# One core, split-precision matmuls: in the first FFN turn the products of each up unit come ahead of the modulation sums, and their columns one unit later

## The reference, cut to what matters

```
c_act = silu(c)
mod = (c_act @ w_ada + b_ada).reshape(bsz, 6, 1024)        # w_ada: 1024 x 6144
shift1, scale1, gate1, shift2, scale2, gate2 = mod[:, 0..5]
u = rms_norm(x, ln1) * (1 + scale1) + shift1
x = x + gate1 * mixer_sublayer(u, ...)
u2 = rms_norm(x, ln2) * (1 + scale2) + shift2
hid = square(relu(u2 @ w_up))                              # w_up: 1024 x 4096
x = x + gate2 * (hid @ w_down)                             # w_down: 4096 x 1024
x = rms_norm(x, final_norm)
second_block(x, ...)                                       # swiglu, attention, swiglu
```

## Time and profile before

| | |
|---|---|
| median of 3 runs | 2444.05 us (2440.28 to 2449.48) |
| the profiled execution, its own time | 2439.08 us |
| span of the profiled execution | 2437.3 us |
| granted TensorE clock, mean | 0.966 |
| busy: TensorE, VectorE, ScalarE | 2303.5, 1344.3, 848.0 us |
| HBM read | 218.56 MB |

### The profile page before, as it was taken

How to read it: one execution, slowest core, us unless ns; L and a number is a source line. 1 busy time by engine, 2 the same in 40 slices (tenths; PEclk the granted TensorE clock), 3 DMA queues, 4 the chain that set the end, 5 groups by cost and what they waited for, 6 DMA issues and landing times.

```text
span 2437.3 us, 28603 instructions
## 1 busy us (share of the span) xinstructions
PE 2303.5 (95%) x10879; PEld 1871.1 (77%) x10879; DVE 1344.3 (55%) x1882; ACT 848.0 (35%) x1192; POOL 0.4 (0%) x6
## 2 busy tenths in 40 slices
PE   4899999999999999999998999999988799999998
PEld 4777777787887797888876888889767667888886
DVE  6646777778574375334346344346668644534444
ACT  1345554553322242222333222225344344222224
POOL 0000000000000000000000000000000000000000
PEclk7799999999999999999999999999999699999999
DMA  6132232232652233323222223222110011223221
GB/s 197 52 122 87 86 100 89 86 102 84 194 182 94 86 104 121 100 91 101 88 86 79 94 87 104 87 95 86 36 61 35 1 35 62 94 88 102 87 93 63
DMA packets 214251, 222.07 MB, mean 91 GB/s; under 512 B 9389, under 2 KB 207466, under 8 KB 213130
## 3 DMA queue, kind: packets, MB, share of 16 engines
q1 hardware_dynamic: 209466, 214.45, 27.2%
q10 hardware_dynamic: 4688, 6.29, 0.8%
HBM read 218.56 MB, written 2.16 MB: 91 GB/s over the span
## 4 chain that ended last, share of the span: by engine, by line
PE 77%; DVE 12%; ACT 6%; issue 4%; DMA 1%; SPq 0%; ACTq 0%; DVEq 0%
PE G L528 21%; PE G L529 21%; PE G L530 21%; PE G L564 2%; PE G L565 2%; PE G L566 2%; PE G L935 1%; ACT whi L1078 1%; PE X L918 1%; DVE rinv L1683 1%; PE X L687 1%; DVE score L2466 1%; ACT seg L1180 1%; DVE m L2465 1%; PE X L952 1%
## 5 line engine op out<-in xcount | busy, mean ns | idle before, releaser
L528 PE MATMUL G<-ahi,whi 128*128 128x512 f32 x1696 | 685.7, 404 | 24.0 <-DVE wlo L1633 9.7
L529 PE MATMUL G<-alo,whi 128*128 128x512 f32 x1696 | 675.7, 398 | 0.0
L530 PE MATMUL G<-ahi,wlo 128*128 128x512 f32 x1696 | 674.9, 398 | 0.0
L1633 DVE TENSOR_TENSOR wlo<-raw,whi 128x2048 fp32r<-128x2048 f32 x177 | 405.6, 2292 | 288.9 <-ACT whi L1078 286.3
L1078 ACT ACTIVATE whi<-raw 128x2048 fp32r<-128x2048 f32 x177 | 337.4, 1906 | 411.4 <-PE G L530 384.1
L528 PEld LDWEIGHTS G<-ahi,whi 128*128 128x128 f32 x1696 | 322.1, 190 | 105.8 <-issue 20.2
L529 PEld LDWEIGHTS G<-alo,whi 128*128 128x128 f32 x1696 | 322.1, 190 | 78.3 <-issue 2.4
L530 PEld LDWEIGHTS G<-ahi,wlo 128*128 128x128 f32 x1696 | 321.3, 189 | 77.2
L529 PE MATMUL G<-hlo,whi 128*128 128x512 f32 x608 | 241.7, 398 | 0.0
L530 PE MATMUL G<-hhi,wlo 128*128 128x512 f32 x608 | 239.6, 394 | 0.0
L528 PE MATMUL G<-hhi,whi 128*128 128x512 f32 x608 | 239.4, 394 | 0.0
(11 more groups left out here) (379 smaller groups left out, 2771.5 us busy)
## 6 DMA issues: line engine op xcount, KB each, us to landing
raw<-in_w_in SPq DMA_DIRECT2D x44, 1024.0 KB, 5.1
raw<-in_w_up SPq DMA_DIRECT2D x38, 1024.0 KB, 5.3
raw<-in_w_down SPq DMA_DIRECT2D x32, 1024.0 KB, 5.1
raw<-in_w_gate SPq DMA_DIRECT2D x22, 1024.0 KB, 5.1
braw<-in_w_ada SPq DMA_DIRECT2D x12, 1024.0 KB, 5.3
raw<-in_w_in SPq DMA_DIRECT2D x18, 512.0 KB, 5.0
bc<-acum_dram SPq DMA_DIRECT2D x8, 1024.0 KB, 6.5
raw<-in_w_ssm_out SPq DMA_DIRECT2D x8, 1024.0 KB, 4.9
```

The source lines that it names most:

```text
L528: pe.matmul(bank[:], wh[:, j, f], rh[:, j, :], start=(j == 0), stop=False)
L529: pe.matmul(bank[:], wh[:, j, f], rl[:, j, :], start=False, stop=False)
L530: last = pe.matmul(bank[:], wl[:, j, f], rh[:, j, :], start=False, stop=(j == k - 1))
L1633: tt(wlo[s][:], raw[s][:], r32(whi[s][:]), ALU.subtract).then_inc(lo_split, 1)
```

## The change

On VectorE the first turn's order becomes: products of unit 0, sum 1, products of unit 1, split of up3, sum 2, products of unit 2, sum 3, split of down0, products of unit 3, sum 4, then `modT` and the split of down1 as before. On TensorE the columns of sum 1 move behind up2, those of sum 2 behind up3, those of sum 3 between the tiles of down0, those of sum 4 behind down0. SyncE's and ScalarE's streams are not edited.

```diff
@@ -811,18 +811,14 @@
                         elif u == 0 and m == 0:
                             half_sum(0, 1)
                 t["op"].add(KB)
+            fm_unit(ahi, alo)
             ada_columns(40, facc)
             fm_unit(ahi, alo)
             ada_columns(42, facc)
             s = next_unit()
-            fm_tile(s, 0, ahi, alo)
-            ada_columns(44, facc)
-            fm_tile(s, 1, ahi, alo)
-            s = next_unit()
             for m in range(2):
                 fm_tile(s, m, hhi, hlo, each=t["op"] if m == 0 else None)
-                if m == 0:
-                    ada_columns(46, facc)
+                ada_columns(44 + 2 * m, facc)
             for _ in range(3):
                 fm_unit(hhi, hlo)
             t["op"].add(KB)
@@ -2176,13 +2172,15 @@
             def ffn_turn(first=False):
 
                 for u in range(4):
-                    if first:
+                    s = early[u] if first and u < 2 else unit()
+                    if first and u == 2:
                         ada_unit(fraw, facc)
-                    s = early[u] if first and u < 2 else unit()
                     for m in range(2):
                         gate_used(s, m)
                         signal(tt(sq[:, m, :], gs[:, m, :], gs[:, m, :], ALU.mult), val_ready, "val")
                         low(hlo[:, 2 * u + m, :], hhi[:, 2 * u + m, :], sq[:, m, :])
+                    if first and u != 1:
+                        ada_unit(fraw, facc)
                 if first:
                     dve.wait_ge(ada_used, 24)
                     link(tt(modT[:, 5, :], X[3][:, 40:48], badaT[:, 40:48], ALU.add))
```

## The result

The changed kernel takes 2453.68 us (median of 20 runs), the kernel before 2443.14 (20 runs): a ratio of 1.0043, 95% interval 1.0028 to 1.0057, so 10.5 us more (7 to 14).

The account below looks back on a forecast made before the run. TensorE was taken as the bound, on the last-ending chain for 77% of the span. Terms: -4.05 - 2.67 (old stall), +12.4 + 2.67 (new stall), +2.7 (second stall), and rounding: 11.1 us more, 2455.2; range 2450 to 2462.

Parts of the forecast that it names:

- The old stall goes: TensorE's 4.05 us idle ahead of up3 and its 2.67 us of lower clock vanish, 6.7 us in all.
- The queue holds down0: SyncE's load of down0 waits behind w_ada unit 23's until sum 2's columns; TensorE idles 12.4 us before down0.
- w_ada 22 is late by nothing: Load of w_ada unit 22, issued near 928.0, lands at 933.0; VectorE asks for it at 933.6.
- modT holds down1: VectorE splits down1 only after modT: 3.19 us from last columns to down1's first product, 2.7 idle.
- The price of the restart: TensorE restarts on the lower clock at down0 after the long idle time, costing 2.67 us.
- my bounds of 1.2 and 2.67: Bounds in us for down0's restart: 2.67 as at 932.40, at least 1.2 as after the idle at 745.38.
- The second fall of the clock: Whether TensorE's clock falls again after the 2.7 us idle before down1: 0 or 1.2 us, left open.
- rival 1: The clock falls a second time, after the idle before down1: 12.3 us more, 2456.4; chance 0.33.
- the main case: The forecast as summed, without a second fall of the clock: 11.1 us more, 2455.2; chance 0.50.
- Rival 2: SyncE's queue order does not bind, down0 lands before it is needed: 3.9 us less, 2440.2; chance 0.04.
- Rival 3: Long idle before down0 costs more than the short: lower clock past first tile or slower transfers, 2459.6; chance 0.11.

## Why the prediction was right

The time was forecast as 11.1 us more, 2455.2; measured are 2453.68, and 10.5 and 11.5 more. The mechanism is the one forecast; that the sum came this close is in part luck, since two of its terms were off in opposite ways. Step by step:

1. *The old stall goes*: right, no idle ahead of up3, and the clock is 1.00 to the end of it.
2. *The queue holds down0*: right, and shown by moving w_ada 23 behind down0 and down1. Of 12.94 us from the columns of sum 2 to down0's first product, 12.96 were taken (939.19 to 952.15), the transfer's 7.7 included.
3. *w_ada 22 is late by nothing*: right; its issue moved to 928.07, sum 3 ran without a wait, and VectorE idled 12.10 us behind it.
4. *modT holds down1*: right, 3.20 us from the columns of sum 4 to the product against 3.19, 2.70 of it idle.
5. *The price of the restart*, 2.67 us, was mis-sized for this profile: down0's first tile took 959.33 - 952.15 = 7.18 us, 1.49 above 5.69. After idle times of the same length it took 7.29 in the second profile of the changed kernel, 6.98 in that with the split ahead of modT and 8.52 in that with TensorE's part alone, so the price after a long idle time is 1.3 to 2.8, and my bounds of 1.2 and 2.67 nearly held it.
6. *The second fall of the clock* was left open and put into rival 1. It came in both profiles of the changed kernel and in that with down0 and down1 loaded first, and not in that with TensorE's part alone, after 2.66 to 2.70 us of idle each. I had put it at 0.33 against 0.50 without it; the runs speak for more. Its price was 1.6 us in the first profile (from 10.0 at down1 to 11.6 at turn 2) against 1.2.

Points 5 and 6 have opposite signs, and by the profile they nearly cancel: -1.2 and +1.6. That is luck. By mechanism, then, rival 1 is what the profiles show, at nearly the time of the main case. Rival 2 is out: the order of the queue binds. Rival 3 is out too: after the long idle time the lower clock cost 1.3 to 2.8 us, about what it cost at most after the short one (2.67, and 2.44 in the second profile of the kernel before), and the transfer took the same 7.7 us.

The Trainium skill's sentence (DMA: Bandwidth & Descriptors, section Anatomy of one DMA) that the wait is the issuing sequencer's fits what was seen: down0's load was issued at 940.13, 0.41 us behind the load that waited. The same section's fit of 2.0 us and bytes over 436e9 a second, which it gives for loads issued from GpSimd, makes down0's 6.4 us as an estimate, where 7.7 were measured on SyncE's queue, and the measurement decides.

## What to carry to other kernels

When work that releases a load is moved later, follow the whole queue of the loads behind that one: a load whose own buffer has long been free waits with it. Order the queue by when each release comes, not by when the data was once wanted, and put a short operation that waits for the end of a chain behind the split or copy that the next unit needs. A stall of 4 us in a profile is worth its own length and the restart of the clock, and removing it pays only if nothing was hanging on the order that made it.

## What was not expected of the hardware

The length of a short idle time did not tell whether the clock falls behind it. An idle time of 2.7 us was followed by the lower clock in three profiles of four, and not in the fourth, that with TensorE's part alone: there 17 products fit into the 4 us behind it.

```profile
982.90:985.40 2.50, 0.02 (x1) 0.02 (x1) 2.36 (x2) 1.45 (x1) 0.00 (x0) 1.00 0.00 0
985.40:989.40 4.00, 4.00 (x17) 3.28 (x18) 3.63 (x3) 0.00 (x0) 0.00 (x0) 1.00 0.75 244
```

In the profile with VectorE's part alone it fell behind an idle time of 1.65 us and not behind those of 2.01 and 1.23; in that of the kernel before it fell behind 2.26 and not behind 3.06. What decides it, no run here shows.

The restart after 11 to 12.6 us of idle was hardly dearer than that after 4 us (1.3 to 2.8 against 2.4 to 2.7).
